# Two reorderings at the start of the x0 stage: VectorE takes x0's first convolutions before its spectrum products, GpSimd a low part between the halves of step 4

## The chip, the cores and the metric
The kernel runs on one core of a Trainium2 chip. The metric is device time in microseconds (us), from a launch of the whole program; lower is better. The engines are called TensorE (PE), VectorE (DVE), ScalarE (ACT), GpSimd (POOL) and SyncE (SP). Each works through its own list of instructions in the order in which they were written, and waits at semaphores for the others.

## What is computed
Two blocks of a model with 512 latent tokens and 256 context tokens, width 1024, in float32. The first block's mixer is an SSD scan beside a Hyena operator; the second's is windowed attention; each is followed by a SwiGLU. The change lies in the Hyena operator of the first block:

```python
def hyena_op(hp, conv_w, conv_b, filt, bias):
    hp = conv_centred(hp, conv_w, conv_b)
    x0, x1, v = jnp.split(hp, 3, axis=-1)
    u = (x1 * v).astype(jnp.float32)
    k = hyena_filter(hp.shape[1], *filt)
    y = long_conv(u, k) + bias.astype(jnp.float32) * u
    return (x0.astype(jnp.float32) * y).astype(hp.dtype)
```

`long_conv` multiplies the spectra of u and k and turns the product back. `hp` is the normed input times a weight matrix, and `conv_centred` a convolution over three tokens.

## The kernel before, in words
Every large product runs at float32 accuracy from three products of rounded operands: with weights W and input H, it adds Whi·Hhi, Wlo·Hhi and Whi·Hlo (lines 516, 517 and 521). So each weight job, two blocks of 128 output columns in halves b = 0 and b = 1, goes through four hands:

1. SyncE loads a half, 512 KB, into one of three slots `W[s]`, as soon as the block that last used that half is done (semaphore `blocks_done`, line 442).
2. DVE rounds it into `WH[b]` (`split_high`, line 1623, called by `next_high`). There is one buffer `WH` for each half, so this waits until TensorE is through with the block before.
3. POOL subtracts, `WL[s] = W[s] - WH[b]` (`low`, line 2146).
4. TensorE waits for that low part (`w_lo`) and multiplies.

Jobs of kind `ada`, which make the modulation vectors, have neither part: they stand in pairs behind each block pair and are multiplied as loaded (line 583).

The x0 stage has four turns n = 0 to 3. In turn n TensorE runs x0's block 2n, something in the middle, block 2n+1, the two `ada` jobs, and something at the end. From n = 1 on, the middle is `inverse(2n-2)` and the end `inverse(2n-1)` (lines 792 and 793), which turn a tile of the spectrum back into tokens. `inverse(j)` waits for `g_ready` to reach j, that is for DVE's `gate(j-1)` (line 1781), which multiplies the tile before by x0 and frees the PSUM region. `inverse(4)` and later need all six spectrum steps.

ACT takes a block out of PSUM with scale and bias (`conv_first`, line 1277). DVE's `conv` (line 1731, four instructions) adds the two neighbouring tokens, and frees the PSUM pair. `x0_conv(n, b)` is such a `conv` and then `next_high`, which rounds half b of turn n+1's weights.

A spectrum step n (0 to 5) is: `spectrum_sums` on DVE (lines 1740, 1741), `spectrum_products(n)` on DVE (lines 1753 to 1757, five instructions into `N4` and `KS`), `spectrum_parts(n, True)` on POOL (lines 2186 to 2189), `spectrum_parts(n, False)` on POOL (line 2194, four instructions). Products n wait for the parts of step n-1 (`p_ready`), as both use `N4`. Steps 0 to 2 are done in an earlier stage; steps 3, 4 and 5 stand at the start of the x0 stage and share DVE and POOL with the rounding of weights. Their order there is written out by hand, and that is what the change edits.

Of the kernel before, what the change touches and what calls it, by code (L numbers as in the profile page):

```python
# [115 lines left out]
def width(g, b):  # L116

    return DOWN[b] if JOBS[g][0] == "down" else HALF
# [7 lines left out]
def along(values, i):  # L126

    if isinstance(i, int):
        return values[i]
    step = values[1] - values[0]  # L130
    assert all(b - a == step for a, b in zip(values, values[1:])), values
    return i * step + values[0]
# [31 lines left out]
def build_kernel(nc, A, out):  # L164
# [6 lines left out]
    with ctx:  # L171
# [157 lines left out]
        def dvec(name, base, i, step=1):  # L329

            at = i * step + (_cols[name] + base)
            return V[:, bass.ds(at, 1)] if not isinstance(at, int) else V[:, at:at + 1]
# [158 lines left out]
        def _(pe):  # L491
# [588 lines left out]
            def score_pair(p):  # L1080

                _, g, b, j, _, lo, nl = unit(2 * p)
                w = nl * P
                cuts = [(0, w, lo * P)] + ([(w, 512, LAT), (512, 640, LAT + P)] if nl == 3 else [(w, 512, LAT)])
                for c, (at0, at1, key) in enumerate(cuts):
                    for e in range(2):
                        if c == 0 and p:
                            pe.wait_ge(at_max, 2 * p - 1 + e)
                        rows = slice(64 * e, 64 * e + 64)
                        ins = mm(PSF[:, 1024 * e + at0:1024 * e + at1], QT[rows, 2 * g + j, b * P:b * P + P],  # L1090
                                 KD[rows, g, key:key + at1 - at0], start=c in (0, 2), stop=c in (len(cuts) - 1, 1))
                        if c == len(cuts) - 1:
                            ins.then_inc(at_s, 1)

            def flip(n):

                _, g, b, j, e, lo, nl = unit(n)
                pe.wait_ge(at_exp, n + 1)
                if n:
                    pe.wait_ge(at_even if n % 2 else at_odd, (n + 1) // 2)  # L1100
                for t in range(nl + 2):
                    ins = pe.transpose(PSF[:, 2048 + t * P:2048 + t * P + P],  # L1102
                                       EX[:, n % 4, 1 + t * P:1 + t * P + P], C[:, IDENT, :])
                ins.then_inc(at_pt, 1)
# [450 lines left out]
        def _(dve):  # L1555
# [153 lines left out]
            def next_high(gs, i, b):  # L1709

                if gs[-1] + 1 < len(JOBS):
                    dve.wait_ge(blocks_done, along([2 * g + 1 + b for g in gs], i))
                    split_high([SPLIT[NTH[g] + 1] for g in gs], i, b)
                    if b == 0 and gs[0] in AFTER_NORM:

                        g = SPLIT[NTH[gs[0]] + 1]
                        dve.wait_ge(w_hi, 2 * NTH[g] + 1)
                        low = W[:, g % SLOTS, 0:HALF, :]
                        TT(WL[:, g % SLOTS, 0:HALF, :], low, WH[:, 0, :, :].bitcast(f32), ALU.subtract) \  # L1719
                            .then_inc(w_lo, 1)  # L1720


            def conv(gs, i, b, wname, n, blk, count, dst=None):

                dve.wait_ge(cv_act, count)
                p, t = pair(PLAN[gs[0]][b][0]), T[:, b, :] if dst is None else dst
                w0, w2 = blk(wname, 0), blk(wname, 2 * n)
                for w, shift in ((w0, -1), (w2, 1)):
                    for j, (lo, hi) in enumerate(SEGS):
                        a, e = (lo + 1, hi) if shift < 0 else (lo, hi - 1)  # L1730
                        ins = STT(t[:, a:e], p[:, a + shift:e + shift], w, t[:, a:e], ALU.mult, ALU.add)  # L1731
                    if shift < 0:
                        ch.link(ins)
                ins.then_inc(pair_free[PLAN[gs[0]][b][0]], 1)

            def spectrum_sums(m, v, bank):

                dve.wait_ge(u_even, m + 1)
                total, diff = (v[1], v[2]) if m % 2 else (v[0], v[3])
                TT(total, diff, PS[:, bank + 1, :], ALU.add)  # L1740
                TT(diff, diff, PS[:, bank + 1, :], ALU.subtract).then_inc(u_sum, 1)

            def spectrum_products(n, v):

                c, f = divmod(n, 3)
                low_f, up = (f, f + 2) if f < 2 else (4, 5)
                cols = slice(512 * c, 512 * c + 512)
                dve.wait_ge(u_sum, 2 * n + 2)
                if n:
                    dve.wait_ge(p_ready, n)  # L1750
                both = lambda x: x.unsqueeze(1).broadcast_to([P, 2, 512])
                k0, k1 = KS[:, :, low_f, cols], KS[:, :, up, cols]
                TT(N4[:, 0:2, :], both(v[0]), k0, ALU.mult)
                TT(N4[:, 3, :], v[2], KS[:, 0, up, cols], ALU.mult)
                ch.link(TT(N4[:, 2, :], v[2], KS[:, 1, up, cols], ALU.mult))
                TT(k0, both(v[1]), k0, ALU.mult)
                TT(k1, both(v[3]), k1, ALU.mult).then_inc(u_prod, 1)
# [11 lines left out]
            def x0_conv(n, b):  # L1769
                g = AT["x0"] + 3 * n  # L1770
                conv([g], 0, b, "hcw", 24, lambda nm, o: dvec(nm, o, 2 * n + b), 16 + 2 * n + b + 1, G[:, 2 * n + b, :])
                next_high([g], 0, b)
# [17 lines left out]
            dve.wait_ge(u_prod, 4)  # L1790
            for m in range(4, 6):
                spectrum_sums(6 + m, US[1], 2 * (m % 3))
            spectrum_products(4, US[0])
            x0_conv(0, 0)
            spectrum_products(5, US[1])
            x0_conv(0, 1)
            for n in range(1, 4):
                x0_conv(n, 0)
                gate(2 * n - 2)
# [310 lines left out]
        def _(pool):  # L2110
# [30 lines left out]
            def low(gs, i, halves=(0, 1)):  # L2141
                s = gs[0] % SLOTS
                for b in halves:
                    at = slice(HALF * b, HALF * b + width(gs[0], b))
                    pool.wait_ge(w_hi, along([2 * NTH[g] + b + 1 for g in gs], i))
                    TT(WL[:, s, at, :], W[:, s, at, :], WH[:, b, 0:width(gs[0], b), :].bitcast(f32),  # L2146
                       ALU.subtract).then_inc(w_lo, 1)

            def following(gs):
                return [SPLIT[NTH[g] + 1] for g in gs]  # L2150
# [28 lines left out]
            def spectrum_parts(n, first):  # L2179

                c, f = divmod(n, 3)
                low_f, up = (f, f + 2) if f < 2 else (4, 5)
                cols = slice(512 * c, 512 * c + 512)
                if first:
                    pool.wait_ge(u_prod, n + 1)
                    TT(N4[:, 0, :], N4[:, 0, :], KS[:, 1, low_f, cols], ALU.subtract)
                    TT(N4[:, 1, :], N4[:, 1, :], KS[:, 0, low_f, cols], ALU.add)
                    TT(N4[:, 3, :], N4[:, 3, :], KS[:, 1, up, cols], ALU.subtract)
                    TT(N4[:, 2, :], N4[:, 2, :], KS[:, 0, up, cols], ALU.add).then_inc(p_half, 1)
                else:  # L2190
                    pool.wait_ge(p_half, n + 1)
                    for odd, op in ((0, ALU.add), (1, ALU.subtract)):
                        for at, k in enumerate((low_f, up)):
                            ins = TT(KS[:, odd, k, cols], N4[:, at, :], N4[:, 2 + at, :], op)
                    ins.then_inc(p_ready, 1)
# [8 lines left out]
            x0 = AT["x0"]  # L2204
            spectrum_parts(3, True)
            spectrum_parts(3, False)
            low(following([x0]), 0, (0,))
            spectrum_parts(4, True)
            spectrum_parts(4, False)
            low(following([x0]), 0, (1,))  # L2210
            spectrum_parts(5, True)
            low(following([x0 + 3]), 0, (0,))
            spectrum_parts(5, False)
# [295 lines left out]
```

## Time and profile before

| | |
|---|---|
| median of 3 runs | 2242.46 us (2240.27 to 2247.51) |
| the profiled execution, its own time | 2243.61 us |
| its span, first to last instruction | 2241.8 us |
| mean granted TensorE clock | 0.967 of full |
| TensorE matmul busy | 2114.9 us, 94% |
| DVE, POOL, ACT busy | 857.2, 810.1, 441.2 us |
| share of the chain that ended last | PE 87%, DVE 5%, POOL 3%, DMA 2%, ACT 2% |

TensorE is busy for 94% of the span, and the chain that ended last runs mostly over it. The rest of the chain lies in places where TensorE waits for another engine. Times below are from the span's start, and the x0 stage's first two turns lie between 328 and 389 us.

### The profile page before, as it was taken

How to read it: one execution, taken by the hardware profiler on the slowest of the kernel's cores; microseconds unless marked ns; L12 is line 12 of the kernel's file. 1: busy time of each engine (PE TensorE's matmuls, PEld its weight loads, DVE VectorE, ACT ScalarE, POOL GpSimd, SP SyncE). 2: the span in 40 equal slices, each digit the busy share in tenths (PEclk: the TensorE clock that was granted, in tenths of full speed). 3: DMA queues.
4: the chain of work that ended last, by engine and by line, in shares of the span. 5: the costliest groups of instructions: out<-in, count | busy, mean ns of one | idle time of the engine just before them, and what ended most of it. 6: DMA issues, size and time to landing. Idle time of an engine off the chain costs nothing.

```text
span 2241.8 us, 29888 instructions
## 1 busy us (share of the span) xinstructions
PE 2114.9 (94%) x11842; PEld 1684.1 (75%) x11842; DVE 857.2 (38%) x1245; ACT 441.2 (20%) x830; POOL 810.1 (36%) x438
## 2 busy tenths in 40 slices
PE   7989998999989978999999999999889999999997
PEld 2477656887877757878888888887676677888886
DVE  4533544212337674332212122233346663322334
ACT  3331110001345551031100001102116602100110
POOL 1443536112227765243223323224310034444443
PEclk9999999999989989999999999998989999999999
DMA  9444323333110011112111211111210022223222
GB/s 385 156 136 140 122 95 114 117 122 116 63 57 1 1 38 52 62 45 69 64 44 65 78 60 65 48 61 61 94 39 1 1 72 74 92 79 114 96 75 76
DMA packets 50791, 182.31 MB, mean 81 GB/s; under 512 B 5568, under 2 KB 6080, under 8 KB 49664
## 3 DMA queue, kind: packets, MB, share of 16 engines
q1 hardware_dynamic: 49600, 171.92, 22.4%
q10 hardware_dynamic: 576, 5.97, 0.7%
q0 software_dynamic: 512, 2.95, 0.4%
q8 instruction: 76, 1.25, 0.2%
q14 instruction: 27, 0.22, 0.0%
HBM read 178.72 MB, written 2.10 MB: 81 GB/s over the span
## 4 chain that ended last, share of the span: by engine, by line
PE 87%; DVE 5%; POOL 3%; DMA 2%; ACT 2%; issue 1%; DVEq 0%; SPq 0%; ACTq 0%
PE psum L516 21%; PE psum L521 21%; PE psum L517 21%; PE psum L1102 2%; PE psum L1090 2%; PE psum L1119 2%; DMA weights<-in_wall 2%; PE psum L583 1%; PE psum L703 1%; PE psum L739 1%; PE psum L918 1%; PE psum L943 1%; PE psum L545 1%; PE psum L666 1%; PE psum L539 1%
## 5 line engine op out<-in xcount | busy, mean ns | idle before, releaser
L2146 POOL TENSOR_TENSOR weights_lo<-weights,weights_hi 128x1024 fp32r<-128x1024 f32 (+1 forms) x228 | 505.1, 2216 | 1012.5 <-DVE weights_hi L1623 1012.5
L521 PE MATMUL psum<-normed_lo,weights_hi 128*128 128x512 f32 x1760 | 508.3, 352 | 0.0
L1623 DVE CAST weights_hi<-weights 128x1024 fp32r<-128x1024 f32 (+1 forms) x232 | 165.6, 715 | 885.5 <-PE psum L521 740.8
L516 PE MATMUL psum<-normed_hi,weights_hi 128*128 128x512 f32 x1088 | 391.5, 360 | 6.7 <-DVE weights_lo L1719 3.9
L517 PE MATMUL psum<-normed_hi,weights_lo 128*128 128x512 f32 x1088 | 373.9, 358 | 0.0
L521 PEld LDWEIGHTS psum<-normed_lo,weights_hi 128*128 128x128 f32 x1760 | 285.4, 190 | 16.5
L516 PEld LDWEIGHTS psum<-normed_hi,weights_hi 128*128 128x128 f32 x1088 | 204.7, 188 | 56.8 <-POOL weights_lo L2146 4.3
L516 PE MATMUL psum<-normed_first_hi,weights_hi 128*128 128x512 f32 (+1 forms) x672 | 233.8, 348 | 11.7 <-POOL weights_lo L2146 8.7
L517 PEld LDWEIGHTS psum<-normed_hi,weights_lo 128*128 128x128 f32 x1088 | 205.4, 189 | 34.9 <-issue 1.0
L517 PE MATMUL psum<-normed_first_hi,weights_lo 128*128 128x512 f32 (+1 forms) x672 | 214.9, 341 | 0.0
L516 PE MATMUL psum<-hidden_hi,weights_hi 128*128 128x512 f32 (+1 forms) x528 | 189.0, 358 | 0.0
L517 PE MATMUL psum<-hidden_hi,weights_lo 128*128 128x512 f32 (+1 forms) x528 | 178.9, 354 | 0.0
L516 PEld LDWEIGHTS psum<-normed_first_hi,weights_hi 128*128 128x128 f32 x672 | 128.8, 192 | 48.2 <-POOL weights_lo L2146 9.8
L521 PE MATMUL psum<-hidden_lo,weights_hi 128*128 128x512 f32 (+1 forms) x528 | 160.4, 358 | 0.0
L517 PEld LDWEIGHTS psum<-normed_first_hi,weights_lo 128*128 128x128 f32 x672 | 128.5, 191 | 16.5 <-issue 1.1
L516 PEld LDWEIGHTS psum<-hidden_hi,weights_hi 128*128 128x128 f32 x528 | 99.1, 188 | 23.4
L517 PEld LDWEIGHTS psum<-hidden_hi,weights_lo 128*128 128x128 f32 x528 | 99.3, 188 | 15.1
L1731 DVE SCALAR_TENSOR_TENSOR temps<-psum,vectors,temps 128x511 f32<-128x511 f32 x112 | 63.8, 612 | 100.1 <-ACT temps L1277 99.1
L1468 ACT ACTIVATE temps<-psum 128x768 f32<-128x768 f32 (+1 forms) x44 | 31.1, 708 | 358.2 <-PE psum L521 353.8
L1472 ACT ACTIVATE hidden_hi<-temps 128x768 f32 (+3 forms) x44 | 32.6, 740 | 332.1 <-DVE temps L2013 332.1
L521 PEld LDWEIGHTS psum<-hidden_lo,weights_hi 128*128 128x128 f32 x528 | 87.1, 188 | 9.0
L516 PE MATMUL psum<-mixed_hi,weights_hi 128*128 128x512 f32 x224 | 76.8, 343 | 8.5 <-POOL weights_lo L2146 8.5
(312 smaller groups left out, 2966.0 us busy)
## 6 DMA issues: line engine op xcount, KB each, us to landing
weights<-in_wall SPq DMA_DIRECT2D x264, 512.0 KB, 3.9
weights<-in_wall SPq DMA_DIRECT2D x32, 384.0 KB, 3.2
weights<-in_wall SPq DMA_DIRECT2D x32, 320.0 KB, 3.0
residual<-in_xT SPq DMA_DIRECT2D x1, 3072.0 KB, 17.3
residual<-in_xT ACTq DMA_DIRECT2D x1, 3072.0 KB, 11.0
phase<-in_tab ACTq DMA_DIRECT2D x2, 1280.0 KB, 5.5
normed<-in_window SPq DMA_DIRECT2D x1, 1536.0 KB, 12.6
normed<-in_window POOLq DMA_DIRECT2D x1, 1536.0 KB, 10.3
```

The costliest lines, as they stand in the source:

```text
L516: mm(acc[:, lo:hi], WH[:, b, k, :], high[:, lo:hi], start=st, stop=False)
L517: mm(acc[:, lo:hi], WL[:, s, HALF * b + k, :], high[:, lo:hi], start=False, stop=False)
L521: ins = mm(acc[:, lo:hi], WH[:, b, k, :], low[:, lo:hi], start=False, stop=en)
L539: mm(accs[b][:, lo:hi], WH[:, b, k, :], high[:, lo:hi], start=k == 0, stop=False)
L1090: ins = mm(PSF[:, 1024 * e + at0:1024 * e + at1], QT[rows, 2 * g + j, b * P:b * P + P], KD[rows, g, key:key + at1 - at0], start=c in (0, 2 ...
L1102: ins = pe.transpose(PSF[:, 2048 + t * P:2048 + t * P + P], EX[:, n % 4, 1 + t * P:1 + t * P + P], C[:, IDENT, :])
L1119: ins = mm(PS[64 * e:64 * e + 64, 6, 0:256].rearrange("p (j c) -> p j c", j=2), VT[:, kt, 64 * g:64 * g + 64], heads_e, start=t == 0, stop ...
L1468: run(T[:, 0, lo:hi], pair(0)[:, lo:hi], ACT.Silu).then_inc(pair_free[0], 1)
L1472: run(at_row(HIDH, r)[:, lo:hi], T[:, 1, lo:hi], ACT.Copy).then_inc(hid_hi, 1)
L1623: dve.tensor_copy(WH[:, b, 0:n, :], W[:, s, HALF * b:HALF * b + n, :]).then_inc(w_hi, 1)
L1731: ins = STT(t[:, a:e], p[:, a + shift:e + shift], w, t[:, a:e], ALU.mult, ALU.add)
L2146: TT(WL[:, s, at, :], W[:, s, at, :], WH[:, b, 0:width(gs[0], b), :].bitcast(f32), ALU.subtract).then_inc(w_lo, 1)
```

## The change
On DVE, `x0_conv(0, 0)` moves from behind `spectrum_products(4)` to before it, and `x0_conv(0, 1)` from behind `spectrum_products(5)` to before it. On POOL, the low part of half 1 of turn 1's job moves from behind the second half of step 4's parts to before it. Nothing is added or left out; no other engine's list changes.

```diff
@@ -1790,10 +1790,10 @@
             dve.wait_ge(u_prod, 4)
             for m in range(4, 6):
                 spectrum_sums(6 + m, US[1], 2 * (m % 3))
+            x0_conv(0, 0)
             spectrum_products(4, US[0])
-            x0_conv(0, 0)
+            x0_conv(0, 1)
             spectrum_products(5, US[1])
-            x0_conv(0, 1)
             for n in range(1, 4):
                 x0_conv(n, 0)
                 gate(2 * n - 2)
@@ -2206,8 +2206,8 @@
             spectrum_parts(3, False)
             low(following([x0]), 0, (0,))
             spectrum_parts(4, True)
+            low(following([x0]), 0, (1,))
             spectrum_parts(4, False)
-            low(following([x0]), 0, (1,))
             spectrum_parts(5, True)
             low(following([x0 + 3]), 0, (0,))
             spectrum_parts(5, False)
```

DVE's list at the first place, behind the spectrum sums of step 5; L1731 is the convolution, L1623 the rounding of the next weights, L1753 the first product of step 4:

```order
 L1740 TENSOR_TENSOR temps<-temps,psum 128x512
 L1741 TENSOR_TENSOR temps<-temps,psum 128x512
+L1731 SCALAR_TENSOR_TENSOR phase<-psum,vectors,phase 128x511
+L1731 SCALAR_TENSOR_TENSOR phase<-psum,vectors,phase 128x255
+L1731 SCALAR_TENSOR_TENSOR phase<-psum,vectors,phase 128x511
+L1731 SCALAR_TENSOR_TENSOR phase<-psum,vectors,phase 128x255
+L1623 CAST weights_hi<-weights 128x1024
 L1753 TENSOR_TENSOR phase<-phase 128x1024
 L1754 TENSOR_TENSOR phase<-phase 128x512
```

The four instructions of block 0's convolution and one rounding now stand ahead of step 4's products. Between step 4's products and step 5's there is still one such group, but it is now that of block 1; behind step 5's products stood two, and now one.

POOL's list at step 4; L2188 and L2189 end the first half of its parts, L2194 is the second half, L2146 a low part of weights, L2186 begins step 5:

```order
 L2188 TENSOR_TENSOR phase<-phase 128x512
 L2189 TENSOR_TENSOR phase<-phase 128x512
-L2194 TENSOR_TENSOR phase<-phase 128x512 x4
-L2146 TENSOR_TENSOR weights_lo<-weights,weights_hi 128x1024
+L2146 TENSOR_TENSOR weights_lo<-weights,weights_hi 128x1024
+L2194 TENSOR_TENSOR phase<-phase 128x512 x4
 L2186 TENSOR_TENSOR phase<-phase 128x512
 L2187 TENSOR_TENSOR phase<-phase 128x512
```

One low part and four instructions of step 4 have changed places.

## Rows read from the trace of the kernel before

**Rows 1.** Waits between 300 and 450 us: us in total, times, longest.

```profile
PE psum L516 <- POOL weights_lo L2146: 8.7, 2, 4.5
```

**Rows 2.** Timeline of PE: start, us, engine, line, operation, count, idle before.

```profile
346.33 1.92 PE L583 MATMUL psum<-weights,phase 128*32 128x512 f32 x16
352.47 0.79 PE L516 MATMUL psum<-normed_first_hi,weights_hi 128*128 128x512 f32 x1 [4.22 <-POOL weights_lo L2146]
...
363.68 0.59 PE L792 MATMUL psum<-phase 128*128 128x256 f32 x2
...
372.68 0.79 PE L516 MATMUL psum<-normed_first_hi,weights_hi 128*128 128x512 f32 x1 [4.50 <-POOL weights_lo L2146]
...
382.56 1.93 PE L583 MATMUL psum<-weights,phase 128*32 128x512 f32 x16
384.41 0.70 PE L792 MATMUL psum<-phase 128*128 128x256 f32 x2
...
388.78 0.48 PE L516 MATMUL psum<-normed_first_hi,weights_hi 128*128 128x512 f32 x1
...
410.05 1.92 PE L583 MATMUL psum<-weights,phase 128*32 128x512 f32 x16
...
437.53 1.92 PE L583 MATMUL psum<-weights,phase 128*32 128x512 f32 x16
```

**Rows 3.** Windows: length, busy us of PE, PEld, DVE, ACT, POOL, clock, DMA share, GB/s.

```profile
348.25:363.68 15.43, 11.21 (x49) 9.69 (x50) 2.87 (x4) 0.00 (x0) 12.29 (x9) 0.78 0.47 160
367.97:382.56 14.59, 10.09 (x51) 8.40 (x50) 6.18 (x12) 0.00 (x0) 12.28 (x8) 0.88 0.00 1
410.12:437.60 27.48, 27.48 (x164) 22.92 (x168) 8.15 (x14) 1.98 (x2) 4.79 (x2) 1.00 0.34 115
```

**Rows 4.** Timeline of DVE.

```profile
342.34 1.23 DVE L1753 TENSOR_TENSOR phase<-phase 128x1024 f32<-128x1024 f32 x1 [7.06 <-POOL phase L2194]
...
347.08 2.31 DVE L1731 SCALAR_TENSOR_TENSOR phase<-psum,vectors,phase 128x511 f32<-128x511 f32 x4
349.31 0.68 DVE L1623 CAST weights_hi<-weights 128x1024 fp32r<-128x1024 f32 x1
...
367.29 2.31 DVE L1731 SCALAR_TENSOR_TENSOR phase<-psum,vectors,phase 128x511 f32<-128x511 f32 x4
...
373.09 1.13 DVE L1781 SCALAR_TENSOR_TENSOR phase<-psum,filter_roots,phase 128x512 f32<-128x512 f32 x2
```

**Rows 5.** Timeline of POOL.

```profile
337.21 5.02 POOL L2194 TENSOR_TENSOR phase<-phase 128x512 f32<-128x512 f32 x4
350.07 2.34 POOL L2146 TENSOR_TENSOR weights_lo<-weights,weights_hi 128x1024 fp32r<-128x1024 f32 x1 [7.84 <-DVE weights_hi L1623]
...
357.42 5.03 POOL L2194 TENSOR_TENSOR phase<-phase 128x512 f32<-128x512 f32 x4
```

**Rows 6.** Timeline of ACT, x0's blocks 0 and 1 leaving PSUM.

```profile
337.17 0.99 ACT L1277 ACTIVATE phase<-psum,vectors 128x768 f32<-128x768 f32 x1 [3.49 <-PE psum L521]
346.43 1.00 ACT L1277 ACTIVATE phase<-psum,vectors 128x768 f32<-128x768 f32 x1 [8.28 <-PE psum L521]
```

**Rows 7.** Weight loads, issue to landing: issued at 337.3; at 346.6; all of them.

```profile
DMA to landing us min/median/max: 3.8/3.8/3.8
...
DMA to landing us min/median/max: 4.4/4.4/4.4
...
DMA to landing us min/median/max: 3.0/3.7/18.3
```

**Rows 8.** Line 1623, 120 to 450 us: duration in ns, min/median/max.

```profile
L1623 DVE CAST weights_hi<-weights x24: 684/696/2201, 136.7 to 441.6; 128x1024 fp32r<-128x1024 f32 x24
```

**Rows 9.** Timelines of POOL and DVE in the output projection.

```profile
878.61 2.41 POOL L2146 TENSOR_TENSOR weights_lo<-weights,weights_hi 128x1024 fp32r<-128x1024 f32 x1 [5.94 <-DVE weights_hi L1623]
...
879.62 2.22 DVE L1599 TENSOR_TENSOR temps<-residual 128x768 f32<-128x768 f32 x1
881.87 0.96 DVE L1600 TENSOR_TENSOR temps<-temps 128x768 f32<-128x768 f32 x1
```

## The prediction, made before the changed kernel ran
> **What bounds the kernel now.** I first read the page: TensorE is busy for 94% of the span, so something helps only where TensorE stands still or runs slow. Next the waits around the change: between 300 and 450 us TensorE waits 8.7 us, in two waits, for low parts of weights from POOL [rows 1]. PE's timeline places them [rows 2]: 4.22 us before turn 1's block 0, which starts at 352.47, and 4.50 us before block 1, at 372.68. The windows show a second cost: in the two stretches that begin with these waits the granted clock is 0.78 and 0.88 of full, and in a later turn 1.00 [rows 3]. So after each wait some matmuls run at 1.2 GHz and not 2.4.
>
> Then I followed each wait back. The low part that block 0 needs runs at 350.07, straight behind DVE's rounding at 349.31 [rows 4, 5]. That rounding stands behind step 4's products (342.34 to 347.08) and a convolution (2.31 us). The products had waited until 342.2 for POOL's parts of step 3 (337.21 + 5.02). Yet ACT had delivered the convolution's input at 338.2 (337.17 + 0.99) [rows 6], and the weights had landed at 337.3 + 3.8 = 341.1 [rows 7]. DVE stood idle for 7.06 us before the products. The second wait is the same once more: parts of step 4 (357.42 + 5.03), products, convolution at 367.29, rounding, low part.
>
> **What the change is worth at most.** From the start of turn 0's `ada` jobs to those of turn 1 takes 382.56 - 346.33 = 36.23 us. The same distance from turn 2 to turn 3 takes 437.53 - 410.05 = 27.48 us without a wait, and holds one `inverse` more, 388.78 - 384.41 = 4.37 us [rows 2]. Without waits and at full clock turn 1 would take 27.48 - 4.37 = 23.11 us. So 13.1 us are there: 8.7 of idle and 4.4 of slow clock.
>
> **Part 1, x0_conv(0, 0) before products 4.** The convolution starts at 338.2 in DVE's idle time and ends at 340.5: nothing. The rounding starts when the weights have landed, 341.1. It takes 0.68 us by itself, up to 2.2 at worst [rows 4, 8]; POOL is in the last instruction of step 3's parts until 342.2. I take the rounding to end at 342.9, after POOL's instruction, and the range of its end is 341.8 to 343.3. Products 4 then start at 342.9 and not 342.34, 0.6 late. The low part for block 0 (2.34) follows the rounding and is ready at 345.3; TensorE asks for it when its `ada` jobs end, 346.33 + 1.92 = 348.25. The 4.22 us wait is gone, with 3.0 us in hand.
>
> **A new neighbour.** Products 4, operations with both inputs in SBUF, now run beside a low part; before, POOL waited for DVE's rounding or products meanwhile. The nearest row for such a pair is in the output projection [rows 9]: line 1599 took 2.22 us while a low part ran until 881.02, and the same size of operation behind it took 0.96. 881.02 + 0.96 = 881.98 is about its end, 881.84: it looks as if DVE's operation had stood still until POOL's was done. At the lower end the products lose nothing; at the upper a whole low part, 2.3 us. I take the upper, as rows 9 are the same kinds of instruction.
>
> The Trainium skill, page "SBUF — State Buffer", section "SBUF: two separate sides", says that a DVE operation with two SBUF inputs and a GpSimd operation that reads SBUF share a port pair by an exclusive lock, whoever comes first, the other waiting for the whole instruction. By it the products or the low part must stand still, which speaks against this reordering; without it the sum is 13.1, with it 12.2, as worked out from rows next. The output projection's rows agree.
>
> **Part 2, x0_conv(0, 1) before products 5, and POOL's low part forward.** Upper end: products 4 end at 342.9 + 4.74 + 2.3 = 350.0 (before: 347.1). Block 1's input leaves ACT at 347.4 [rows 6]. The convolution runs 350.0 to 352.3, and its weights landed at 346.6 + 4.4 = 351.0 [rows 7]. The rounding waits for one of POOL's instructions and ends near 353.3. POOL's first half of step 4 takes from 350.1 to 355.7 (5.0 and 0.6 for the rounding), the low part until 358.1, the second half until 363.1. Block 1 wants that low part when block 0 (8.45 us: 27.48 less the `ada` jobs' 1.85 and two `inverse`, halved) and `inverse(0)` are through: 348.3 + 8.45 + 4.4 = 361.1. It is there 3.0 us early; the 4.50 us wait is gone too.
>
> Products 5 then run 363.2 to 367.9 (before: 362.55 to 367.29). **What is late next** is `gate(0)`: convolution until 370.3, rounding until 371.3 (one instruction of POOL's in its way), gate 1.13 us [rows 4] until 372.4. TensorE reaches `inverse(1)` at 361.1 + 8.45 + 1.9 = 371.5. So there is a wait of 0.9 us. At the lower end, with no standing still, `gate(0)` ends at 370.1 and nothing waits.
>
> POOL's next low parts: first half of step 5 until 373.7, low part until 376.1, wanted at 372.4 + 4.4 = 376.8; the other about 383.5, wanted at 389.6. Each fits. SyncE's list is unchanged; its loads follow `blocks_done`. In turn 1 they come as they do in turns 2 and 3, at the same pace, where TensorE does not wait. `inverse(4)` needs step 5's second half, done by 381, and is not reached before turn 3.
>
> **Sum.** 13.1 saved, 0.9 given back: 12.2 us. The profiled execution (span 2241.8, own time 2243.61, 1.15 above the median) would be 2231.4. Behind the stage every start is set by an event that moves with TensorE, so I carry the gain through whole: 2242.46 - 12.2 = 2230.3 us. A measurement of this kernel can tell about 0.3%, 6.7 us, from no change.
>
> **Rivals.**
> *No standing still (lower end):* products 4 take 4.74 us beside the low part, nothing waits at `inverse(1)`: 2229.4 us. For it: no row shows products and a low part beside each other. Against: the pair in [rows 9]. Chance 25%.
> *A part comes back later:* `gate(0)` or a low part is 3 to 5 us late, for instance since DVE's operations stand still for each of POOL's and not for one; then TensorE waits at `inverse(1)`, with 1 to 2 us of slow clock behind it (before, 4.4 for two waits): from 2242.46 - 13.1 + 3 + 1 = 2233.4 to 2236.4, in the middle 2234.9. For it: only 0.9 us lie between the lists. Against: the margins of 3.0 at both low parts. Chance 12%.
> *A late load (slower):* DVE's rounding now stands ahead of step 4's products, and the rounding waits for its load. It decides nothing while the load lands by 342. If it took as long as the longest load in the trace, 18.3 us [rows 7], it would land at 355.6. The low part ends 358.7, TensorE has waited 10.4 us and lost 2.7 of clock. Products 4 run to 364.1, parts and low part to 372.2, second half to 377.2, products 5 to 382.1, `gate(0)` to 386.6, where `inverse(1)` started at 384.41 before: 2.2 later, 2244.7 us. The point from which it is slower is a load of some 16 us. Against: this load took 3.8, the median is 3.7 and its issue is moved by nothing. Chance 2%, most of it within 0.3% of no change.
> *The change does nothing:* that needs the low parts to have been bound elsewhere. The lists differ as described, and the idle DVE time is in the row; 1%, 2242.5 us.
>
> **Numbers.** Forecast as summed 60%, the rivals 25, 12, 2 and 1. Range: from 2225.5, the lower end's 2229.4 less the 2.2 by which the fastest run shown lies under the median and some for the clock's later changes, up to 2235.5, below which most of "comes back later" lies. Faster by over 0.3% (below 2235.7): the first two cases and two thirds of the third, 0.93. Within 0.3%: the last third, no effect, and most of the late load, 0.06. Slower by more: a load still later, 0.01.
>
> **What would show it.** Right: no wait of TensorE for POOL's low parts between 346 and 390; clock 1.00 there; roundings near 341 to 343 and 352 to 353; one product of step 4 near 2.3 us longer; from one `ada` start to the next 24.0 us in place of 36.23; `inverse(1)` waiting under 1 us for `gate(0)`. Wrong: a wait left at either block, products 4 held back by the rounding beyond 343.5, or a distance of 24 us and a total that has not moved by 12: then the gain was lost behind the stage.

## The result and the profile after

The changed kernel takes 2228.05 us, median of 7 runs (2224.75 to 2233.93), beside 2243.24 for the kernel before (7 runs, 2240.27 to 2247.51). The ratio is 0.9933, 95% interval 0.9919 to 0.9947: 15 us faster, between 12 and 18. The forecast was 2230.3 us. The profiled execution took 2231.30 us, with a span of 2229.5; forecast for it was 2231.4.

Both waits for low parts are gone. This is PE's timeline of the changed kernel, for [rows 2]; its times from the span's start are 0.86 us earlier than before's already ahead of the change (345.47 for 346.33), so what follows compares distances or takes 0.86 off the forecast's times:

```profile
345.47 1.93 PE L583 MATMUL psum<-weights,phase 128*32 128x512 f32 x16
347.33 0.50 PE L516 MATMUL psum<-normed_first_hi,weights_hi 128*128 128x512 f32 x1
...
355.81 0.59 PE L792 MATMUL psum<-phase 128*128 128x256 f32 x2
...
360.07 0.48 PE L516 MATMUL psum<-normed_first_hi,weights_hi 128*128 128x512 f32 x1
...
368.62 1.92 PE L583 MATMUL psum<-weights,phase 128*32 128x512 f32 x16
371.01 0.70 PE L792 MATMUL psum<-phase 128*128 128x256 f32 x2 [0.47 <-DVE phase L1781]
...
383.85 0.59 PE L792 MATMUL psum<-phase 128*128 128x256 f32 x2
```

From the start of turn 0's `ada` jobs (L583) to `inverse(1)`, the last L792 row before turn 2, it now takes 371.01 - 345.47 = 25.54 us; before it was 384.41 - 346.33 = 38.08. I call this distance the **stretch**, as each experiment below is read by it. It is 12.54 us shorter. The one wait left in it is for DVE's `gate(0)`. The clock in it, by the windows view with the columns of [rows 3]:

```profile
345.50:371.00 25.50, 25.04 (x153) 19.39 (x152) 15.59 (x22) 2.97 (x3) 16.95 (x12) 1.00 0.41 134
```

TensorE is at full clock throughout. Now DVE, for [rows 4]:

```profile
337.34 2.31 DVE L1731 SCALAR_TENSOR_TENSOR phase<-psum,vectors,phase 128x511 f32<-128x511 f32 x4 [2.92 <-ACT phase L1277]
340.08 0.70 DVE L1623 CAST weights_hi<-weights 128x1024 fp32r<-128x1024 f32 x1 [0.42 <-DMA weights<-in_wall]
342.02 3.35 DVE L1753 TENSOR_TENSOR phase<-phase 128x1024 f32<-128x1024 f32 x1 [1.24 <-POOL phase L2194]
345.29 0.68 DVE L1754 TENSOR_TENSOR phase<-phase 128x512 f32<-128x512 f32 x1
...
348.88 2.31 DVE L1731 SCALAR_TENSOR_TENSOR phase<-psum,vectors,phase 128x511 f32<-128x511 f32 x4
351.10 1.04 DVE L1623 CAST weights_hi<-weights 128x1024 fp32r<-128x1024 f32 x1
361.92 1.22 DVE L1753 TENSOR_TENSOR phase<-temps,phase 128x1024 f32<-128x1024 f32 x1 [9.77 <-POOL phase L2194]
...
369.83 1.13 DVE L1781 SCALAR_TENSOR_TENSOR phase<-psum,filter_roots,phase 128x512 f32<-128x512 f32 x2
```

And POOL, for [rows 5]:

```profile
336.36 5.56 POOL L2194 TENSOR_TENSOR phase<-phase 128x512 f32<-128x512 f32 x4
341.88 2.40 POOL L2146 TENSOR_TENSOR weights_lo<-weights,weights_hi 128x1024 fp32r<-128x1024 f32 x1
...
354.50 2.38 POOL L2146 TENSOR_TENSOR weights_lo<-weights,weights_hi 128x1024 fp32r<-128x1024 f32 x1
356.85 4.96 POOL L2194 TENSOR_TENSOR phase<-phase 128x512 f32<-128x512 f32 x4
```

Convolution and rounding of block 0 fill DVE's old idle time. The first product of step 4 starts 0.14 us behind POOL's low part and takes 3.35 us where it took 1.23: it ends 1.1 us after that low part (345.37 against 344.28). The low parts are ready at 344.28 and 356.88, and TensorE starts the blocks that need them at 347.33 and 360.07, without a wait: 3 us in hand each time.

The last `ada` job starts at 514.2 in place of 527.6, 13.4 earlier, and the last matmul 12.3 earlier; 0.9 of each was there ahead of the change. So of the stretch's 12.5 us this pair of profiles still has 12.5 at the last `ada` job and 11.5 at the end. One pair cannot say what becomes of the last microsecond; the profiles of the experiments, compared under "What stays open", move by more than that.

### The profile page after: what moved, and what is told of

Same layout as the page of the kernel before. It is cut to its first block, busy times and chain, and to the rows that moved or that the text cites. A ratio compares the mean times of both kernels' runs of the same rounds, so it can differ in the third digit from the quotient of the medians.

```text
span 2229.5 us, 29888 instructions
## 1 busy us (share of the span) xinstructions
PE 2111.7 (95%) x11842; PEld 1682.1 (75%) x11842; DVE 860.5 (39%) x1245; ACT 441.2 (20%) x830; POOL 811.3 (36%) x438
## 4 chain that ended last, share of the span: by engine, by line
PE 87%; DVE 5%; POOL 3%; ACT 2%; DMA 2%; issue 1%; DVEq 0%; ACTq 0%; SPq 0%
PE psum L516 21%; PE psum L521 21%; PE psum L517 21%; PE psum L1102 2%; PE psum L1090 2%; PE psum L1119 2%; PE psum L583 1%; PE psum L703 1%; DMA weights<-in_wall 1%; PE psum L739 1%; PE psum L918 1%; PE psum L539 1%; PE psum L545 1%; PE psum L943 1%; PE psum L540 1%
## 5 line engine op out<-in xcount | busy, mean ns | idle before, releaser
L2146 POOL TENSOR_TENSOR weights_lo<-weights,weights_hi 128x1024 fp32r<-128x1024 f32 (+1 forms) x228 | 504.9, 2215 | 989.4 <-DVE weights_hi L1623 989.4
L1623 DVE CAST weights_hi<-weights 128x1024 fp32r<-128x1024 f32 (+1 forms) x232 | 166.7, 720 | 887.1 <-PE psum L521 741.4
L1731 DVE SCALAR_TENSOR_TENSOR temps<-psum,vectors,temps 128x511 f32<-128x511 f32 x112 | 63.8, 612 | 99.2 <-ACT temps L1277 98.3
```

The costliest lines, as they stand in the source:

```text
L1623: dve.tensor_copy(WH[:, b, 0:n, :], W[:, s, HALF * b:HALF * b + n, :]).then_inc(w_hi, 1)
```

## The experiments

All were timed beside the kernel before. The first four share one set of runs of before (median 2245.41), the last three another (2245.03).

### Only x0_conv(0, 0) forward

Against the kernel before, on DVE:

```diff
-            spectrum_products(4, US[0])
             x0_conv(0, 0)
+            spectrum_products(4, US[0])
             spectrum_products(5, US[1])
             x0_conv(0, 1)
```

> VectorE takes x0_conv(0, 0) before products 4, everything else as before the change. Theory of the prediction (one chain: rounding, low part, parts, products): the 4.2 us wait of TensorE before turn 1's block 0 goes, but block 1's rounding still stands behind products 5 (which end near 364), convolution and rounding end at 367, the low part at 369.3, and TensorE now asks for it at 360. So it waits 9.2 us there, and its block 1 starts at 369.4 where it started at 372.7 before: nearly all of the first wait's 7 us is given back, and the whole is 2 to 4 us faster than before. Rival (each reordering is worth its own wait): the second wait stays at 4.5 us and the whole is 7 us faster.

Measured: 2240.74 us (11 runs), ratio 0.9979, interval 0.9969 to 0.9988. PE's timeline:

```profile
346.55 1.93 PE L583 MATMUL psum<-weights,phase 128*32 128x512 f32 x16
...
370.34 0.80 PE L516 MATMUL psum<-normed_first_hi,weights_hi 128*128 128x512 f32 x1 [8.95 <-POOL weights_lo L2146]
...
380.85 1.93 PE L583 MATMUL psum<-weights,phase 128*32 128x512 f32 x16
382.71 0.70 PE L792 MATMUL psum<-phase 128*128 128x256 f32 x2
```

The first wait is gone and the second has grown from 4.50 to 8.95 us. The stretch is 382.71 - 346.55 = 36.16 us, 1.9 shorter than before. The rival's 7 us are ruled out by the wait: a wait moved is not a wait removed, as long as the next low part hangs on the same chain.

### Only x0_conv(0, 1) forward, with POOL's low part

Against the changed kernel, on DVE:

```diff
-            x0_conv(0, 0)
             spectrum_products(4, US[0])
+            x0_conv(0, 0)
             x0_conv(0, 1)
             spectrum_products(5, US[1])
```

> VectorE runs products 4, x0_conv(0, 0), x0_conv(0, 1), products 5; GpSimd's low part of half 1 stands between the halves of step 4 as in the changed kernel. Theory: the wait before block 0 stays at 4.2 us with its slow clock, products 4 run beside no low part and take 4.7 us, the wait before block 1 goes, and gate(0), near 374, is in time for inverse(1) at 378.5, where it started at 384.4 before: 6 us faster than before. Rival (the first reordering is what makes the second possible): block 1's low part comes late and a wait of 3 us or more stays before it, 2 to 3 us faster.

Measured: 2237.08 us (5 runs), ratio 0.9964, interval 0.9950 to 0.9978. PE and DVE:

```profile
347.08 1.92 PE L583 MATMUL psum<-weights,phase 128*32 128x512 f32 x16
353.25 0.80 PE L516 MATMUL psum<-normed_first_hi,weights_hi 128*128 128x512 f32 x1 [4.25 <-POOL weights_lo L2146]
...
379.14 0.70 PE L792 MATMUL psum<-phase 128*128 128x256 f32 x2
```

```profile
343.12 1.23 DVE L1753 TENSOR_TENSOR phase<-phase 128x1024 f32<-128x1024 f32 x1 [7.08 <-POOL phase L2194]
344.26 0.68 DVE L1754 TENSOR_TENSOR phase<-phase 128x512 f32<-128x512 f32 x1
```

The first wait stands at 4.25, the second is gone, and the stretch is 32.06, 6.0 shorter than before, as the theory had it. The products run beside no low part and take their 1.23 and 0.68. So `x0_conv(0, 0)` forward by itself is worth 1.9 us in the stretch, `x0_conv(0, 1)` forward with GpSimd's low part 6.0, and all three moves together 12.5. `x0_conv(0, 1)` without GpSimd's move, and GpSimd's move alone, were not run.

### VectorE's reordering without GpSimd's

Against the changed kernel, on POOL:

```diff
             spectrum_parts(4, True)
-            low(following([x0]), 0, (1,))
             spectrum_parts(4, False)
+            low(following([x0]), 0, (1,))
```

> VectorE's list as in the changed kernel, GpSimd's as before: the low part of half 1 stands behind the second half of step 4. Theory: that low part ends at 361.9 where the changed kernel has it at 356.9; TensorE asks for it at 360.1 and waits 1.8 us before block 1. Products 5 start 2.3 us earlier (359.6), so the wait of 0.5 us for gate(0) goes. inverse(1) starts near 372.3, 1.3 us later than in the changed kernel: 11 us faster than before. Rival (GpSimd's move carries much of the gain): a wait of 4 us or more before block 1 and slow clock behind it, 7 us faster than before.

Measured: 2232.23 us (6 runs), ratio 0.9934, interval 0.9918 to 0.9950. PE, then DVE:

```profile
345.06 1.92 PE L583 MATMUL psum<-weights,phase 128*32 128x512 f32 x16
...
361.44 0.50 PE L516 MATMUL psum<-normed_first_hi,weights_hi 128*128 128x512 f32 x1 [1.54 <-POOL weights_lo L2146]
...
370.02 1.93 PE L583 MATMUL psum<-weights,phase 128*32 128x512 f32 x16
371.87 0.70 PE L792 MATMUL psum<-phase 128*128 128x256 f32 x2
```

```profile
341.46 1.21 DVE L1753 TENSOR_TENSOR phase<-phase 128x1024 f32<-128x1024 f32 x1
342.60 2.88 DVE L1754 TENSOR_TENSOR phase<-phase 128x512 f32<-128x512 f32 x1
...
359.19 3.28 DVE L1753 TENSOR_TENSOR phase<-temps,phase 128x1024 f32<-128x1024 f32 x1 [7.54 <-POOL phase L2194]
```

The stretch is 26.81 us, 1.27 longer than in the changed kernel and 11.3 shorter than before; the wait before block 1 is 1.54. So GpSimd's move, added to DVE's two, is worth 1.3 us, and the rival that saw much of the gain there falls; in the medians the move can't be told. One thing I had not expected: products 5, now at the same time as the low part, stand still too, 3.28 us for the first.

### Low part and products kept apart

Against the changed kernel, on POOL (`u_prod` counts the sets of products that are through, so 5 means those of steps 0 to 4):

```diff
+            pool.wait_ge(u_prod, 5)
             low(following([x0]), 0, (0,))
             spectrum_parts(4, True)
```

> The changed kernel, with GpSimd's low part of half 0 held until products 4 are through, so that the two no longer run beside each other. Theory (VectorE's product stands still for as long as the low part runs): the first product of step 4 takes 1.2 us and not 3.35, products 4 end 2.1 us sooner (near 346.9), the low part runs from 346.9 to 349.3, GpSimd's parts of step 4 begin at 349.3 as in the changed kernel, and TensorE waits 1.5 to 2 us before block 0: 1 to 2 us slower than the changed kernel. Rival (the product took 3.35 us for another reason, such as its place behind the rounding): it takes 3.35 us again, the low part ends at 351.5, TensorE waits 4 us, and the whole is 5 us or more slower than the changed kernel.

Measured: 2234.05 us (5 runs), ratio 0.9946, interval 0.9932 to 0.9960. DVE, POOL and PE:

```profile
341.97 1.21 DVE L1753 TENSOR_TENSOR phase<-phase 128x1024 f32<-128x1024 f32 x1
343.11 0.68 DVE L1754 TENSOR_TENSOR phase<-phase 128x512 f32<-128x512 f32 x1
```

```profile
346.86 2.35 POOL L2146 TENSOR_TENSOR weights_lo<-weights,weights_hi 128x1024 fp32r<-128x1024 f32 x1 [5.36 <-DVE phase L1757]
349.17 1.30 POOL L2186 TENSOR_TENSOR phase<-phase 128x512 f32<-128x512 f32 x1
```

```profile
345.57 1.92 PE L583 MATMUL psum<-weights,phase 128*32 128x512 f32 x16
349.27 0.50 PE L516 MATMUL psum<-normed_first_hi,weights_hi 128*128 128x512 f32 x1 [1.77 <-POOL weights_lo L2146]
...
372.41 0.70 PE L792 MATMUL psum<-phase 128*128 128x256 f32 x2
```

With the low part out of the way the same products in the same place take 1.21 and 0.68 us. They end 2.2 us sooner, POOL's parts of step 4 begin when they did (349.17 for 349.04), and TensorE waits 1.77 us. The stretch is 26.84, 1.3 longer than in the changed kernel. The standing still is shown, and it is cheaper to bear it than to avoid it: POOL has to do both pieces before DVE's step 5 in any case.

### The changed kernel again

> The changed kernel once more, to narrow its ratio. Theory: the stretch from turn 0's ada jobs to inverse(1) takes 25.5 us again where it took 38.1 before; what the medians show beyond these 12.5 us comes from stretches outside, whose times move from execution to execution, so the ratio comes nearer to 0.9944 (12.5 us) than to 0.9933. Rival: the change also shortens something outside the stage; then the ratio stays at 0.9933 or below and one later stretch is shorter in this profile as in the first.

Measured: 2230.71 us (6 runs), ratio 0.9940, interval 0.9923 to 0.9957. The stretch is 372.07 - 346.64 = 25.43 us, 12.65 shorter than before. The ratio came nearer to the stretch's 12.5 us (0.9944), which lies in both intervals. Between the two profiles of this one kernel the start of the SSD stage, read against each profile's own start of the stretch, lies 1.7 us apart, and the last matmul of line 521, read the same way, 0.1 us; the medians hold such movements too.

One thing differs inside the stretch. Here the weights landed later, and DVE's rounding took 1.55 us and not 0.70, so that the product was ahead of POOL's low part. DVE:

```profile
341.54 1.55 DVE L1623 CAST weights_hi<-weights 128x1024 fp32r<-128x1024 f32 x1 [0.71 <-DMA weights<-in_wall]
343.01 1.21 DVE L1753 TENSOR_TENSOR phase<-phase 128x1024 f32<-128x1024 f32 x1
344.14 2.88 DVE L1754 TENSOR_TENSOR phase<-phase 128x512 f32<-128x512 f32 x1
```

The low part took 3.31 us, from 343.17. The same kernel can run in either order, and the stretch is the same within 0.1 us.

### gate(0) before products 5 too

Against the changed kernel, on DVE (the loop behind leaves the two out):

```diff
             x0_conv(0, 1)
+            x0_conv(1, 0)
+            gate(0)
             spectrum_products(5, US[1])
```

> The changed kernel with x0_conv(1, 0) and gate(0) too before products 5, in the 9.8 us in which VectorE stands idle there. Theory: the block's input is there at 357, the next weights near 359 to 360, inverse(0) ends at 360.2, so the gate ends near 361.4, before GpSimd's parts at 361.9; products 5 start where they did, the 0.5 us wait before inverse(1) goes, and the stretch takes 25.1 us and not 25.5: 0.5 us faster than the changed kernel, which the medians can't tell. Rival (the load or inverse(0) comes late and now holds products 5): products 5 start 1 us or more later, GpSimd's low part for the next turn with them, and a wait of 1 us or more appears before turn 2's block: 1 to 4 us slower than the changed kernel.

Measured: 2231.24 us (6 runs), ratio 0.9946, interval 0.9929 to 0.9963. DVE, then PE (GpSimd's line 2194 is 2197 in this file):

```profile
359.03 1.13 DVE L1781 SCALAR_TENSOR_TENSOR phase<-psum,filter_roots,phase 128x512 f32<-128x512 f32 x2
360.36 1.23 DVE L1753 TENSOR_TENSOR phase<-temps,phase 128x1024 f32<-128x1024 f32 x1 [0.20 <-POOL phase L2197]
```

```profile
343.53 1.92 PE L583 MATMUL psum<-weights,phase 128*32 128x512 f32 x16
...
366.67 1.93 PE L583 MATMUL psum<-weights,phase 128*32 128x512 f32 x16
368.53 0.70 PE L792 MATMUL psum<-phase 128*128 128x256 f32 x2
```

The gate ends 0.2 us before products 5 can start, the wait before `inverse(1)` is gone, and the stretch is 25.00 us, 0.5 shorter than in the changed kernel. The medians (2231.24 and 2230.71 in the same set) can't tell half a microsecond, so this is no version that is shown to be faster; it shows that nothing is left to wait for in the stretch.

### A rounding that comes 8 us late

Against the changed kernel, on DVE, with x0_conv(0, 0) written as its two parts:

```diff
-            x0_conv(0, 0)
+            conv([AT["x0"]], 0, 0, "hcw", 24, lambda nm, o: dvec(nm, o, 0), 17, G[:, 0, :])
+            for _ in range(10):
+                ch.link(dve.memset(T[:, 3, :], 0.0))
+            next_high([AT["x0"]], 0, 0)
```

> The changed kernel with ten linked memsets of 128x768 between the convolution of block 0 and the rounding behind it, 7 to 8 us of VectorE's time, as a load that lands 8 us late would do. Theory (one chain from this rounding over products, parts and products to gate(0), with next to no margin): the rounding ends near 348.5, TensorE waits 4 us before block 0 and runs slow for a while, the chain moves by 7 us, and inverse(1) starts 7 us later than in the changed kernel, though the low part alone had 3 us in hand: 6 to 8 us slower than the changed kernel, 5 to 6 faster than before. Rival (the idle time of VectorE and GpSimd further on takes up the delay): the chain catches up, inverse(1) starts 3 us later or less.

Measured: 2238.44 us (12 runs), ratio 0.9974, interval 0.9961 to 0.9987. PE's timeline (the low part is the same call, three lines further down in this file):

```profile
345.88 1.92 PE L583 MATMUL psum<-weights,phase 128*32 128x512 f32 x16
353.30 0.80 PE L516 MATMUL psum<-normed_first_hi,weights_hi 128*128 128x512 f32 x1 [5.50 <-POOL weights_lo L2149]
...
376.22 1.92 PE L583 MATMUL psum<-weights,phase 128*32 128x512 f32 x16
378.85 0.70 PE L792 MATMUL psum<-phase 128*128 128x256 f32 x2 [0.70 <-DVE phase L1781]
```

And DVE's rounding:

```profile
349.23 0.69 DVE L1623 CAST weights_hi<-weights 128x1024 fp32r<-128x1024 f32 x1
```

It ended at 349.92, read from the start of the stretch 8.7 us later than in the changed kernel; I had put it near 348.5, but ten linked memsets cost 0.93 us each. The stretch is 32.97 us, 7.4 longer than in the changed kernel. The chain does not catch up. The first 1.2 us of delay cost nothing, as in the changed kernel the products wait for POOL from 340.78 to 342.02 anyway; the other 7.5 are passed on whole, to 0.1 us. This stands in for the late load of the rivals: at 8.7 us of delay the kernel is still faster than before.

## Why the prediction was right

- **What is there to gain.** Forecast 13.1 us, measured 13.1: from `ada` start to `ada` start the changed kernel takes 368.62 - 345.47 = 23.15 for 36.23, where the turn without waits had been put at 23.11. My list of signs said 24.0 for this distance. That was a slip: the wait for `gate(0)` lies behind the second `ada` start and does not belong in it.
- **Part 1.** The first product of step 4 was to start 0.6 us late; it was 0.5 (342.02 against 342.34 - 0.86). The way there was not the one I gave. The rounding did not wait for POOL's instruction; it ran at once in 0.70 us, and POOL's four instructions took 5.56 and not 5.02. In the second profile of this kernel, and in the kernels with `x0_conv(0, 0)` alone, without GpSimd's move and with the two kept apart, the rounding took 1.55 to 1.70 us, as forecast, and POOL's four 5.02 or 5.03.
- **A new neighbour.** Taken at a whole low part, 2.3 us; the first product took 2.12 us more, and the set of five ended at 348.97, forecast 350.0 - 0.86 = 349.1. The lower bound of this term, with its rival of 25%, is ruled out by that product and by the kernel with the two kept apart. The time alone could not have done it: 2228.05 us lies nearer to that rival's 2229.4 than to the 2230.3 of the sum.

The Trainium skill, page "SBUF — State Buffer", section "SBUF: two separate sides", has the loser of the shared port pair wait for a whole instruction; this case's traces agree, with 3.35 us beside a low part and 1.21 without, and with POOL as the loser as well (below).

- **Part 2.** Second low part ready at 356.88 (forecast 358.1 - 0.86 = 357.2), products 5 at 361.92 (362.3), end of `gate(0)` at 370.96 (371.5), and its wait 0.47 us for a forecast of 0.9. Every step came 0.3 to 0.6 us early.
- **Sum.** 12.2 forecast, 12.54 in the stretch, 12.3 in the profiled spans and 15 in the ratio, with 12 as the lower end of its interval; the second measurement gave 13.5 (9.7 to 17.3). The forecast carried the gain through whole. That held up to the SSD stage; whether it holds to the end, the traces do not show (below).
- **Rivals.** A part that comes back later did not appear in the changed kernel. It did in the kernel with one convolution alone: 7 us won at the first wait and 5 given back at the second. A late rounding costs one for one beyond a margin of 1.2 us, as the late load's rival had it. That rival's own sum has a slip of 0.8 us: from a rounding that ends at 356.3, products 4 end at 356.3 + 4.74 + 2.3 = 363.3 and not at 364.1, so that `gate(0)` comes out 1.4 us and not 2.2 behind before.

**What stays open.** In seven of the eight comparisons with before, those of the changed kernel included, the ratios show more than the stretch, by 0.7 to 3.5 us; in the eighth, less by 1.0. The sets share runs of before, so these are not eight independent signs, and in all but one (x0_conv(0, 0) alone: 1.9 us in the stretch, 2.7 to 7.0 by its interval) the stretch's gain lies within the interval. The profiles do not bear this surplus out. Counted from the start of the stretch, the SSD stage (line 928) starts earlier than before by what the stretch gained, within 0.1 us in six of the eight profiles and with 1.5 us more in two (the changed kernel again and `x0_conv(0, 1)` with the low part). Counted to the last matmul of line 521, at the kernel's end, 11.5 and 11.6 us are left in the two profiles of the changed kernel, and in the others the gain is between 3.7 us less and 3.0 us more than in the stretch; for `x0_conv(0, 0)` alone nothing is left. All of them are held against one profile of the kernel before. So what the stages behind make of the gain is open, in both directions.

## What to carry to other kernels

Follow each wait of the busy engine back to the first moment at which its inputs were all there: here a rounding could have run 8 us sooner, in idle time of the engine that had it behind other work. Then ask what the next wait hangs on before adding up gains. When two waits are fed by one chain, removing the first alone moves most of its time to the second (1.9 us left of 7). Removing the second alone paid in full here (6.0 us, for a wait of 4.50 and 1.4 of slow clock behind it), and both together 12.5 of 13.1.

## What the runs showed of the hardware

**DVE's products and POOL's low part stand still for each other, in either order.** In the first profile of the changed kernel POOL's low part started 0.14 us ahead and took 2.40 us, and DVE's product took 3.35. In the kernel with `x0_conv(0, 0)` alone the product came first. POOL:

```profile
343.09 3.31 POOL L2146 TENSOR_TENSOR weights_lo<-weights,weights_hi 128x1024 fp32r<-128x1024 f32 x1 [0.63 <-DVE weights_hi L1623]
```

and DVE:

```profile
342.93 1.21 DVE L1753 TENSOR_TENSOR phase<-phase 128x1024 f32<-128x1024 f32 x1
344.07 2.89 DVE L1754 TENSOR_TENSOR phase<-phase 128x512 f32<-128x512 f32 x1
```

The low part took 3.31 us, 0.96 more than its 2.35, and ended at 346.40; the product before it ran free in 1.21, and the one behind it, 0.68 by itself, took 2.89. So these two take turns instruction by instruction, and one low part costs DVE's list some 2.1 us whichever comes first. Not every DVE instruction does this. The convolution, which reads one input from PSUM, took 2.31 us at 348.88 in the changed kernel, with POOL's parts of step 4 beside it from 349.04, and 2.31 us at 347.08 in the kernel before, with POOL idle. Behind it the rounding took 1.04 us for 0.68, and the POOL instruction beside it 1.74 for 1.29.

**A short wait cost no slow clock here, and behind the long ones the price did not follow the length.** Without a wait the changed kernel's two blocks took 8.48 and 8.55 us (the forecast had 8.45). Behind a wait of 1.77 us a block took 8.47 (349.27 to `inverse(0)` at 357.74), and behind one of 1.54, 8.58, both at a granted clock of 1.00. Behind 4.22 and 4.50 us it took 11.21 and 9.88 [rows 2], behind 4.25, 11.24 (353.25 to 364.49), behind 5.50, 10.12 (353.30 to 363.42), and behind 8.95, 10.51. The granted clock of these five blocks was 0.73, 0.85, 0.73, 0.82 and 0.80: part of each ran at 1.2 GHz and not 2.4. So the two short waits cost their own length, and the long ones 1.4 to 2.8 us more, the longest of them not the most.
